# First layer: the q product from tokens without their shift, and the shift's part added as a product of its own

## The chip, the cores and the metric

The kernel runs on one core of a Trainium2 chip. The metric is the device time of one execution in microseconds (us). Engines are named as in the profile: PE (TensorE matmul), PEld (its weight loads), DVE (VectorE), ACT (ScalarE), POOL (GpSimd), SP (the queue that issues the weight DMAs).

## The reference, cut to what matters

Two token streams of 256 tokens by 1024 channels, x and ctx, pass through the first layer. The kernel goes on through expert layers and a second block; the change touches the first layer's start.

```python
sh1, sc1, g1, sh2, sc2, g2 = split(silu(c) @ ada_w[0] + ada_b[0], 6)   # 1024 -> 6 x 1024; c for x, c_ctx for ctx
h = rms_norm(x, norm_mix[0]) * (1 + sc1) + sh1                       # shift sh1, scale sc1
proj = h @ ev_w_in                                                   # q 512 | k 512 | v 512 | z 512 | gates 16 | pool 512
qkv = silu(dw_conv(proj[:, :1536], conv_w))                          # conv of width 3 over tokens
# q and z, pool only of x; k, v and the gates of both streams
```

The convolution is linear and q is linear in h, so q = (h without shift) @ w + (shift @ w), the second term being the same for every token.

## The kernel before, in words

Activations lie with channels on the partitions: `hT` is 8 tiles k of 128 channels by 512 columns, 0 to 255 for x and 256 to 511 for ctx. Weights stream in chunks of 2 MB (1024 rows by 512 columns), issued by SP in the order of the list `stream` (L443 to L453) into a ring of four slots; a chunk waits for the release of the one that held its slot four places earlier. The 24 chunks `ada_w` give the modulation vectors: `ada_mm` (L603) is a product with 32 columns (in the profile 16 matmul records at L613), ACT copies its bank to `PART` (`ada_copy`, L1707), `ada_turn` (L618) transposes it on PE in four pieces (L571), and `ada_bias` (L2230) sums and adds the bias on DVE into `MOD`. The first four chunks hold shift tiles 0 to 3, shift 4 to 7, scale 0 to 3, scale 4 to 7. SP waits for x and ctx, loaded by the ACT queue (L1628), before it issues the third (L1464 to L1466).

Order of the start: ACT squares the tokens, DVE finishes the root and scales them (L2287 to L2294), PE turns them into `hT` (L639 to L644), and PE does four ada products with their turns (L638, L645 to L650). DVE then scales and shifts the eight x tiles (L2310). The q product reads them: two quarters (m = 0, 1; a quarter is 128 output columns) as plain f32 products (L680), two as three products each of split operands (`first_product`, L669). A split operand is a high part in fp32r made by ACT and a low part, the rest, made by DVE: for weights `high` (L1610, 128x1024) and `split` (L2188, 128x1024), for the tokens L1725 and L1731 on ACT and `first_low` (L2314) on DVE. The first quarter of k, over 512 columns, needs the split of all 16 token tiles. ACT also scales and shifts the ctx tiles of `hT` (L1736), which the gates' product reads later.

Behind it, `late_vectors` (L652) turns some vectors, `ada_step` (L662) does an ada product, and k, v, z, pool follow, with an `ada_step` between each. For each output tile t ACT copies the bank to `CB` (L1759), DVE convolves it: one `tensor_scalar` (L2339) and two `scalar_tensor_tensor` (L2182), then ACT applies silu. DVE does the weights' low part and this work in one fixed order (L2329 to L2343). The mixer's order is written out in `mixer_steps` (L69); its step `ada_product` is an `ada_step`. POOL makes masks at the start and waits from L1545 for the mixer.

## Time and profile before

| | us |
|---|---|
| median of 3 runs (1290.58 to 1293.01) | 1290.7 |
| the profiled execution's own time | 1291.09 |
| its span, first to last instruction | 1289.1 |
| PE busy in the span | 1121.6 (87%) |
| DVE busy | 630.3 (49%) |
| ACT busy | 452.4 (35%) |
| POOL busy | 78.4 (6%) |

Times in rows are microseconds from the span's start. A timeline row has start, length, engine, line, operation, out<-in, shapes and the count of merged instructions; in brackets the idle time before it and what ended it. A length can overlap the next start, since an engine begins an instruction before the one in front has left it. A groups row has busy time, and the mean of one in ns. PEclk 1.00 is 2.4 GHz and 0.50 is 1.2 GHz.

### The profile page before, as it was taken

Reading aid. Unit: us, or ns where it says so; the run is one execution under the profiler, and the core shown is the slowest. Engines: PE = TensorE matmul, PEld = TensorE weight load, DVE = VectorE, ACT = ScalarE, POOL = GpSimd, SP = SyncE. Lnnn points to the kernel's source line nnn. Section 1 sums busy time; section 2 is a strip of 40 time slices with the busy share of each in tenths; the row PEclk is TensorE's granted clock in tenths of the full one; section 3 lists DMA queues with packets and bytes.
Section 4 is the critical chain, followed back from the end, with each engine's and each line's share of the span. In section 5 each row is a group of like instructions: output and inputs, shape, how many; then the busy total and the mean of one; then the engine's idle time right before and its main releaser. Section 6 shows DMA issues by size and latency. Waiting matters only on the chain.

```text
span 1289.1 us, 19518 instructions
## 1 busy us (share of the span) xinstructions
PE 1121.6 (87%) x8166; PEld 840.5 (65%) x8166; DVE 630.3 (49%) x1175; ACT 452.4 (35%) x835; POOL 78.4 (6%) x118
## 2 busy tenths in 40 slices
PE   5899999999996757589999766669999999999998
PEld 2677667896842313169995222316899879999886
DVE  4655876656530102056654010103886378656774
ACT  3535534322410000034332000002565668453553
POOL 3000124540000000000000000000100000000000
PEclk8999999999998878899999887879999999999999
DMA  9937766109989999995778999999454313453300
GB/s 325 337 131 264 276 227 217 67 15 390 420 345 421 421 421 421 420 384 178 291 289 335 421 420 421 422 421 391 137 196 143 126 60 132 146 181 131 131 18 33
DMA packets 104187, 339.17 MB, mean 263 GB/s; under 512 B 7849, under 2 KB 10774, under 8 KB 81574
## 3 DMA queue, kind: packets, MB, share of 16 engines
q1 hardware_dynamic: 97408, 334.51, 66.9%
q10 hardware_dynamic: 6694, 3.43, 1.0%
q8 instruction: 65, 1.06, 0.3%
q14 instruction: 20, 0.16, 0.0%
HBM read 336.88 MB, written 1.05 MB: 262 GB/s over the span
## 4 chain that ended last, share of the span: by engine, by line
PE 62%; DMA 15%; SPq 10%; DVE 8%; ACT 3%; issue 2%; ACTq 0%; DVEq 0%
PE bank L708 8%; PE bank L710 8%; PE bank L709 8%; SPq L1439 5%; SPq L1450 4%; PE bank L1072 4%; PE bank L613 3%; DMA arena<-in_w_gate_dram 3%; DMA arena<-in_w_up_dram 3%; DMA weight_ring<-in_w_up_dram 3%; DMA weight_ring<-in_w_gate_dram 3%; DVE arena L2179 2%; DMA weight_ring<-in_w_down_dram 2%; PE bank L690 2%; PE bank L691 2%
## 5 line engine op out<-in xcount | busy, mean ns | idle before, releaser
L2179 DVE TENSOR_TENSOR weights_low<-weight_ring,weights_high 128x1024 fp32r<-128x1024 f32 x150 | 183.4, 1224 | 121.9 <-ACT weights_high L1621 121.4
L1621 ACT ACTIVATE weights_high<-weight_ring 128x1024 fp32r<-128x1024 f32 x150 | 158.3, 1057 | 192.5 <-PE bank L710 179.2
L708 PE MATMUL bank<-input_high,weights_high 128*128 128x272 f32 (+1 forms) x672 | 195.2, 290 | 4.8 <-DVE input_low L2179 2.3
L710 PE MATMUL bank<-input_high,weights_low 128*128 128x272 f32 (+1 forms) x672 | 191.8, 285 | 0.0
L709 PE MATMUL bank<-input_low,weights_high 128*128 128x272 f32 (+1 forms) x672 | 191.3, 285 | 0.0
L708 PEld LDWEIGHTS bank<-input_high,weights_high 128*128 128x128 f32 x672 | 126.6, 188 | 9.2 <-issue 4.9
L2179 DVE TENSOR_TENSOR arena<-arena,bank 128x512 f32<-128x512 f32 (+1 forms) x38 | 24.6, 651 | 219.8 <-PE bank L1072 206.4
L710 PEld LDWEIGHTS bank<-input_high,weights_low 128*128 128x128 f32 x672 | 126.8, 189 | 0.0
L709 PEld LDWEIGHTS bank<-input_low,weights_high 128*128 128x128 f32 x672 | 126.5, 188 | 0.1
L708 PE MATMUL bank<-raw_high,weights_high 128*128 128x272 f32 (+1 forms) x320 | 93.1, 291 | 2.0 <-DVE weights_low L2179 2.0
L710 PE MATMUL bank<-raw_high,weights_low 128*128 128x272 f32 (+1 forms) x320 | 91.2, 285 | 0.0
L1072 PE MATMUL bank<-weight_ring,arena 128*32 128x512 f32 x448 | 61.6, 692 | 28.0 <-DMA weight_ring<-in_w_up_dram 18.1
L1072 PE MATMUL bank<-arena 128*32 128x512 f32 x384 | 57.5, 744 | 27.1 <-DMA arena<-in_w_up_dram 16.7
L709 PE MATMUL bank<-raw_low,weights_high 128*128 128x256 f32 (+1 forms) x256 | 72.8, 284 | 0.0
L2179 DVE TENSOR_TENSOR arena<-arena 128x272 f32<-128x272 f32 (+12 forms) x94 | 52.7, 568 | 20.8 <-ACT arena L2007 9.0
L708 PEld LDWEIGHTS bank<-raw_high,weights_high 128*128 128x128 f32 x320 | 60.1, 188 | 3.7 <-DVE weights_low L2179 3.2
L710 PEld LDWEIGHTS bank<-raw_high,weights_low 128*128 128x128 f32 x320 | 60.3, 188 | 0.0
L1072 PEld LDWEIGHTS bank<-weight_ring,arena 128*32 128x32 f32 x448 | 16.0, 125 | 67.2 <-issue 65.3
L613 PE MATMUL bank<-weight_ring,silu_c 128*32 128x512 f32 x384 | 49.2, 633 | 11.4 <-DMA weight_ring<-in_ada_w_dram 11.4
L1072 PE MATMUL bank<-expert_slots,arena 128*32 128x512 f32 x192 | 33.8, 866 | 28.3 <-DMA expert_slots<-in_w_up_dram 18.4
L2182 DVE SCALAR_TENSOR_TENSOR arena<-arena,vectors 128x272 f32<-128x272 f32 (+2 forms) x106 | 56.9, 539 | 2.9
L2182 DVE SCALAR_TENSOR_TENSOR residual<-bank,modulation,residual 128x256 f32<-128x256 f32 x80 | 36.1, 484 | 42.1 <-PE bank L998 25.7
(469 smaller groups left out, 1970.6 us busy)
## 6 DMA issues: line engine op xcount, KB each, us to landing
weight_ring<-in_ada_w_dram SPq DMA_DIRECT2D x24, 2048.0 KB, 10.2
weight_ring<-in_w_gate_dram SPq DMA_DIRECT2D x16, 2048.0 KB, 24.5
arena<-in_w_down_dram SPq DMA_DIRECT2D x16, 2048.0 KB, 32.7
arena<-in_w_gate_dram SPq DMA_DIRECT2D x12, 2048.0 KB, 21.6
arena<-in_w_up_dram SPq DMA_DIRECT2D x12, 2048.0 KB, 33.0
weight_ring<-in_w_up_dram SPq DMA_DIRECT2D x12, 2048.0 KB, 27.5
weight_ring<-in_even_w_in_dram SPq DMA_DIRECT2D x9, 2048.0 KB, 9.0
expert_slots<-in_w_up_dram SPq DMA_DIRECT2D x8, 2048.0 KB, 32.7
```

Of the source, the lines that this page charges most:

```text
L613: mm = pe.matmul(b[j:j + 32, :], CS[:, 2 * k:2 * k + 32], w[:, k, :], start=k < 4, stop=k >= 4)
L690: pe.matmul(b[:, 0:width], hi[:, k, :], XHI1[:, k, 0:width], start=k == 0, stop=False)
L691: pe.matmul(b[:, 0:width], hi[:, k, :], XLO1[:, k, 0:width], start=False, stop=False)
L708: pe.matmul(b[:, 0:width], hi[:, k, :], high[:, k, t0:t0 + width], start=k == 0, stop=False)
L709: pe.matmul(b[:, 0:width], hi[:, k, :], low[:, k, t0:t0 + width], start=False, stop=False)
L710: mm = pe.matmul(b[:, 0:width], lo[:, k, :], high[:, k, t0:t0 + width], start=False, stop=k == KD - 1)
L1072: mm = pe.matmul(b[32 * e:32 * e + 32, :], XG[:, 2 * q + k, 32 * e:32 * e + 32], w[e][:, k if by_quarter else 2 * (q % 2) + k, :], start=q ...
L1439: sp.dma_start(dst, src).then_inc(landed[slot_of(cn)], 16)
L1450: sp.dma_start(dst.rearrange("p (e n) -> p e n", e=2), src).then_inc(landed[slot_of(cn)], 16)
L1621: act.activation(WHI[:, j % 2], quarter_of(j), ACT.Copy).then_inc(weights_high, 1)
L2179: return dve.tensor_tensor(out_, a, b, op)
L2182: return dve.scalar_tensor_tensor(out_, a, s, b, op0, op1)
```

## The change

The scale chunks are loaded first, then q's weights, then ctx (by SP, in two DMAs), then the two shift chunks. Token work is done stream by stream. DVE only scales the x tiles; q's four quarters are all plain f32 products of unshifted tokens. Behind the third quarter PE turns the ctx tokens and does the two shift products; the token split with the shift folded in (ACT `Identity` with bias, DVE `scalar_tensor_tensor`) starts then, under the fourth. `shift_product` multiplies the shift with q's weights, which keeps q's slot until then; the result is copied, turned, summed and added by DVE to the four q tiles in `CB` ahead of their convolution. The shift is added to `hT` itself by POOL, in four operations of 128x1024, behind the whole split. The small DMAs (gates' weights and two vectors) move from 16 us to behind the split on ACT's queue. The ada step ahead of k goes behind k's second quarter. In the mixer, an `ada_product` does its product first and the turn of the one before it behind that; the last warm-up of PE is put ahead of the last turn.

```diff
-        stream = ada_src[0:4]
+        ada_order = [2, 3, 0, 1] + list(range(4, 24))
-        for src in ((ev, 0), (ev, 512), None, (ev, 1024), None, None, (ev, QKV), (ev, QKV + 512 + 16), None, None, None):
+        for src in (None, None, (ev, 0), None, None, (ev, 512), None, (ev, 1024), None, None, (ev, QKV), (ev, QKV + 512 + 16),
+                    None, None, None):
...
-            ada_mm()
-            for tt in range(2 * TT):
...
-            for i in range(3):
+            for tt in range(TT):
+                token_turns(tt)
+            for i in range(2):
+                warm(3)
                 ada_mm()
-                pe.wait_ge(scalar_drained, ada["copied"] - 1)
-                ada_turn()
-            pe.wait_ge(scalar_drained, ada["copied"])
-            ada_turn()
+                ada_turn_now()
...
+            def ada_step(turn_behind=False):
+                copied, turned = ada["copied"], ada["turned"] < ada["next"]
+                if turn_behind:
+                    ada_mm()
+                if turned:
+                    pe.wait_ge(scalar_drained, copied)
                     ada_turn()
+                if not turn_behind:
+                    ada_mm()
...
-                        if (i, m) in ((0, 2), (1, 0)):
-                            pe.wait_ge(first_split, KD * i + k + 1)
+                        if (i, m) == (1, 0):
+                            pe.wait_ge(first_split, 2 * k + 2)
...
+            def unshifted_product(between):
+                cn = W_EV[0]
+                arrive(cn)
+                for m in range(4):
+                    b = s_open()
+                    for k in range(KD):
+                        if m == 0:
+                            pe.wait_ge(h_scaled, k + 1)
+                        mm = pe.matmul(b[:, 0:T], chunk(cn)[:, k, m * P:m * P + P], hT[:, k, 0:T], start=k == 0, stop=k == KD - 1)
+                    s_close(mm, ("qkv", m))
+                    between(m)
+            def shift_product():
+                cn = W_EV[0]
+                pe.wait_ge(shift_ready, 2)
+                shifts = MOD[:, 0, :, :].rearrange("p c r -> p (c r)")
+                b = s_open()
+                for k in range(KD):
+                    j = 32 * (k % 4)
+                    mm = pe.matmul(b[j:j + 32, :], shifts[:, 2 * k:2 * k + 32], chunk(cn)[:, k, :], start=k < 4, stop=k >= 4)
+                released[cn] = (scalar_filled, s_close(mm, "shift_parts"))
...
+            def after_q(m):
+                if m == 2:
+                    for tt in (2, 3):
+                        token_turns(tt)
+                    ada_mm()
+                    ada_mm()
+                    pe.wait_ge(scalar_drained, ada["copied"] - 1)
+                    ada_turn()
+                if m == 3:
+                    ada_turn_now()
+            def after_k(m):
+                if m == 0:
+                    shift_turn()
+                if m == 1:
+                    ada_step()
             warm(4)
-            first_product(0, 0, T, s_open, s_close, "qkv")
+            unshifted_product(after_q)
             late_vectors()
-            ada_step()
-            first_product(1, 4, 2 * T, s_open, s_close, "qkv")
+            shift_product()
+            first_product(1, 4, 2 * T, s_open, s_close, "qkv", between=after_k)
...
-                    ada_step()
+                    ada_step(turn_behind=kind == "ada_product")
...
+            warm(3)
             pe.wait_ge(scalar_drained, ada["copied"])
             ada_turn()
...
+            pool.wait_ge(first_split, 2 * KD)
+            for r in range(2):
+                for k in (0, 4):
+                    h = hT[:, k:k + 4, r * T:r * T + T]
+                    pool.tensor_tensor(h, h, last(MOD[:, 0, k:k + 4, r], T), ALU.add).then_inc(h_shifted, 1)
...
+            act.wait_ge(shift_ready, 1)
+            act.wait_ge(context_scaled, 1)
             for k in range(KD):
+                if k == 2:
+                    high()
+                if k == 4:
+                    conv_input(3, 1)
+                    b = take()
+                    drained(act.activation(XH[:, :, 0:META], bank(b, KD, META), ACT.Copy))
+                    act.wait_ge(shift_ready, 2)
+                for r, done in enumerate((h_ready, context_high)):
+                    s = slice(r * T, r * T + T)
+                    act.activation(XHI1[:, k, s], hT[:, k, s], ACT.Identity, bias=MOD[:, 0, k, r:r + 1]).then_inc(done, 1)
+                if k == 4:
+                    b = take()
+                    drained(act.activation(QBP, b[:, :], ACT.Copy))
             high()
...
+            h = hT[:, :, T:2 * T]
+            tt(h, h, last(gain[:, :, 1], T), MUL).then_inc(context_scaled, 1)
             for k in range(KD):
+                if k % 4 == 0:
+                    ada_bias(shift_ready, k // 4 + 1)
+                if k == 2:
+                    split()
                 first_low(k, 0, h_ready)
+                first_low(k, 1, context_high)
             split()
             vec_copies((1, 2))
             tt(gain_sq, vec("norm_final", 0, 8), vec("norm_final", 0, 8), MUL)
+            b = take()
+            parts = b[:, :].rearrange("p (f q s) -> p f s q", f=4, q=4)[:, :, 0, :]
+            drained(dve.reduce_sum(QB, parts, AX.X), True)
+            dve.wait_ge(scalar_drained, mark[("qkv", 3)])
+            v = CB[:, :, 0, 1:1 + T]
+            then(tt(v, v, last(QB, T), ADD))
             for t in range(12):
-                if t >= 3:
+                if t == 2 or t > 4:
                     split()
```

## Rows read from the trace of the kernel before

**Rows 1.** The chain that ended last, 0 to 62 us: start, length, what
```profile
12.38 22.51 DMA weight_ring<-in_ada_w_dram
...
34.93 3.24 PE bank L613 x16
```
**Rows 2.** Busy by stretch: PE, PEld, DVE, ACT, POOL, PEclk, DMA share, GB/s
```profile
59.00:81.40 22.40, 22.40 (x103) 17.95 (x105) 14.79 (x22) 7.69 (x13) 0.00 (x0) 1.00 0.46 167
...
121.70:145.00 23.30, 23.30 (x175) 16.53 (x175) 15.77 (x47) 11.78 (x22) 0.00 (x0) 1.00 0.45 153
```
**Rows 3.** Timeline of PE, first 42 us
```profile
19.62 4.15 PE L571 MATMUL bank<-ident,arena 128*128 128x128 f32 x32
...
28.57 1.92 PE L613 MATMUL bank<-weight_ring,silu_c 128*32 128x512 f32 x16 [2.36 <-DMA weight_ring<-in_ada_w_dram]
...
34.93 3.24 PE L613 MATMUL bank<-weight_ring,silu_c 128*32 128x512 f32 x16 [3.85 <-DMA weight_ring<-in_ada_w_dram]
...
39.50 0.66 PE L571 MATMUL bank<-ident,ada_partials 128*128 128x128 f32 x4 [0.75 <-ACT ada_partials L1711]
39.99 2.00 PE L579 MATMUL bank<-upper_then_ones 128*128 128x272 f32 x8
41.83 7.07 PE L680 MATMUL bank<-arena,weight_ring 128*128 128x256 f32 x32
```
**Rows 4.** One stretch, PE alone: length, PE busy, PEclk, DMA share, GB/s
```profile
32.00:36.00 4.00, 1.07 (x8) 0.78 1.05 387
```
**Rows 5.** Timeline of DVE, first 60 us
```profile
10.44 1.29 DVE L2226 COPY residual<-bank 128x512 f32<-128x512 f32 x2 [0.16 <-PE bank L597]
...
14.81 2.78 DVE L2294 TENSOR_SCALAR arena<-arena 128x1024 f32<-128x1024 f32 x4
...
57.15 0.35 DVE L2339 TENSOR_SCALAR arena<-arena,vectors 128x256 f32<-128x256 f32 x1
57.53 1.01 DVE L2182 SCALAR_TENSOR_TENSOR arena<-arena,vectors 128x256 f32<-128x256 f32 x2
```
**Rows 6.** DMA issues, 15 to 25 us (q's chunk, issued 19.75): KB, us to landing
```profile
weight_ring<-in_ev_w_in_dram SPq DMA_DIRECT2D x1, 2048.0 KB, 20.6
```
**Rows 7.** Timeline of PE: k's first product, its last, v's first
```profile
58.31 0.50 PE L690 MATMUL bank<-first_input_high,weights_high 128*128 128x512 f32 x1
...
80.57 0.40 PE L692 MATMUL bank<-first_input_high,weights_low 128*128 128x512 f32 x1
...
83.19 0.50 PE L690 MATMUL bank<-first_input_high,weights_high 128*128 128x512 f32 x1
```
**Rows 8.** Groups by form: the operations of the splits and convolutions
```profile
L2179 DVE TENSOR_TENSOR weights_low<-weight_ring,weights_high 128x1024 fp32r<-128x1024 f32 x150 | 183.4, 1224 | 121.9 <-ACT weights_high L1621 121.4
L1621 ACT ACTIVATE weights_high<-weight_ring 128x1024 fp32r<-128x1024 f32 x150 | 158.3, 1057 | 192.5 <-PE bank L710 179.2
...
L1658 ACT ACTIVATE input_high<-arena,modulation 128x256 fp32r<-128x256 f32 x8 | 3.3, 495 | 1.3 <-DVE arena L2182 1.3
...
L2182 DVE SCALAR_TENSOR_TENSOR input_low<-arena,modulation,input_high 128x256 fp32r<-128x256 f32 x8 | 3.3, 481 | 0.0
...
L2182 DVE SCALAR_TENSOR_TENSOR arena<-arena,vectors 128x512 f32<-128x512 f32 x16 | 12.0, 752 | 0.6
```
**Rows 9.** POOL beside DVE in the mixer: a group, then timeline rows
```profile
L1568 POOL TENSOR_TENSOR arena<-arena,small 128x512 f32<-128x512 f32 x8 | 8.5, 1064 | 0.0
...
245.72 1.05 POOL L1568 TENSOR_TENSOR arena<-arena,small 128x512 f32<-128x512 f32 x1
245.94 1.38 DVE L2179 TENSOR_TENSOR arena<-arena,small 128x512 f32<-128x512 f32 x1
246.73 1.61 POOL L1563 TENSOR_TENSOR arena<-backward_direction,arena 128x512 f32<-128x512 f32 x1
...
253.96 0.68 DVE L2179 TENSOR_TENSOR arena<-arena,small 128x512 f32<-128x512 f32 x1
```
**Rows 10.** Timeline of PE in the mixer: a turn that waits for its copy
```profile
196.16 0.66 PE L571 MATMUL bank<-ident,ada_partials 128*128 128x128 f32 x4 [0.72 <-ACT ada_partials L1711]
```

More of the change, by code:

```diff
@@ L1463, in _ @@
                     sp.wait_ge(first_vec_in, 16 * len(first_vecs))
-                if cn == 2:
-                    sp.wait_ge(x_in, 16)
-                    sp.wait_ge(ctx_in, 16)
+                if cn == 3:
+                    for i in range(TT):
+                        sp.dma_start(XIN[TT + i], ctx[0][i * P:i * P + P, :]).then_inc(ctx_in, 16)
                 free_slot(cn)
@@ L1508, in _ @@
             then(pool.memset(GW[:, KD, :], 0.0))
+            then(pool.memset(MOD[:, 0, :, :], 0.0))
             pool.iota(SLOTN, pattern=[[1, CAP]], base=1, channel_multiplier=0,
@@ L1627, in _ @@
                 act.dma_start(VEC[r:r + k, g, :], vec_src[name]).then_inc(first_vec_in, 16)
[L1628 to L1629 removed]
+            for i in range(TT):
+                act.dma_start(XIN[i], x[0][i * P:i * P + P, :]).then_inc(x_in, 16)
             logs()
@@ L1718, in _ @@
                     drained(act.activation(hT[:, 4 * kh:4 * kh + 4, tt * P:tt * P + P], bank(b, 4, P), ACT.Copy))
-            for _ in range(3):
-                ada_copy()
-            for k in range(KD):
-                scaled_tiles[0] += 1
-                act.wait_ge(h_scaled, scaled_tiles[0])
-                act.activation(XHI1[:, k, 0:T], hT[:, k, 0:T], ACT.Copy).then_inc(h_ready, 1)
-            high()
-            high()
-            for half in range(2):
-                ks = range(4 * half, 4 * half + 4)
-                for k in ks:
-                    act.activation(XHI1[:, k, T:2 * T], hT[:, k, T:2 * T], ACT.Identity, scale=gain[:, k, 1:2],
-                                   bias=MOD[:, 0, k, 1:2]).then_inc(context_high, 1)
-                act.wait_ge(context_high, 4 * half + 4)
-                for k in ks:
-                    h = hT[:, k, T:2 * T]
-                    act.activation(h, h, ACT.Identity, scale=gain[:, k, 1:2], bias=MOD[:, 0, k, 1:2]).then_inc(context_scaled, 1)
@@ L1737, in _, with conv_input @@
-            high()
+            def conv_input(t, w):
+                b = take()
+                drained(act.activation(CB[:, t % 4, 0:w, 1:1 + T], bank(b, w, T), ACT.Copy))
+            hidden_tokens(1)
+            for _ in range(2):
+                ada_copy()
+            act.wait_ge(edges_ready, 1)
+            conv_input(0, 1)
+            act.wait_ge(ctx_in, 16 * TT)
+            token_squares_of(1, context_squares)
+            conv_input(1, 1)
+            conv_input(2, 1)
+            hidden_tokens(3)
@@ L2236, in ada_bias @@
                 drained(dve.reduce_sum(MODS, parts, AX.X), True)
-                then(tt(MOD[:, ly, c0:c0 + 4, :], MODS, last(vec("ada_b", 48 * ly + c0, 4), 2), ADD))
+                ins = tt(MOD[:, ly, c0:c0 + 4, :], MODS, last(vec("ada_b", 48 * ly + c0, 4), 2), ADD)
+                if signal is None:
+                    then(ins)
+                else:
+                    ins.then_inc(signal, 1)
+                    dve.wait_ge(signal, value)
                 ada[0] += 1
@@ L2298, in _, with first_low @@
                     drained(dve.tensor_copy(hT[:, 4 * kh:4 * kh + 4, t_ * P:t_ * P + P], bank(b, 4, P)))
-            for i in range(4):
+            def first_low(k, r, signal):
+                dve.wait_ge(signal, k + 1)
+                s = slice(r * T, r * T + T)
+                stt(XLO1[:, k, s], hT[:, k, s], MOD[:, 0, k, r:r + 1], XHI1[:, k, s].bitcast(F32), ADD, SUB).then_inc(first_split, 1)
+            token_roots(0)
+            for _ in range(2):
                 ada_bias()
```

150 lines of the change are left out of this document (71 added, 79 removed).

## The prediction

> **What bounds the kernel now.** I read the chain of waits first, since the change lies in the first 80 us. There the end is set by the load of the fourth modulation chunk, which lands at 34.9, and by its product on PE [rows 1]. Next the stretches: from 59 us to 145 us PE is busy without a gap at 2.4 GHz [rows 2], so whatever moves v's first product earlier moves everything behind it, and the one number to forecast is that start. It is at 83.19; k runs from 58.31 to 80.8 [rows 7], 5.6 us a quarter, and an ada step of turn and product (2.4 us) follows. So k starts 23 us after the chunk has landed, and the time between goes to q, to the split of 16 token tiles and to an ada step.
>
> The sum is made against the profiled execution, 1291.09 us (span 1289.1); that is 0.4 above the median, so a difference found here is put on 1290.7.
>
> **First part: until q may start.** In the new order two chunks and x stand ahead of q's weights. q's chunk lands at 19.75 + 20.6 = 40.35 [rows 6], four 2 MB chunks, x and ctx (1 MB each) having come before; a chunk takes some 5.4 us (34.9 to 40.35). Counted back from that, the second scale chunk lands near 19, q's near 25, the last shift chunk, which has the place that q had, at 40.35. PE: DVE is free at 11.73 (10.44 + 1.29), finishes the root in 0.8 and scales the first tile in 0.70; 16 turns follow from 13.3, 0.13 to 0.2 us each (4.15 for 32), to 16.5 [rows 3, 5]. A warm-up of three is 1.4 (eight records take 1.85 without the tail), an ada product 1.85, its copy and turn 1.16 (PE idles 0.72 of it [rows 10]). Twice 4.4 us gives 25.4; the warm-up of four ends at 27.25, and q starts. DVE's gain and first scaled tile are ready at 26.6.
>
> **Second part: until the split may start.** A plain quarter is 3.4 us (7.07 for two, less 0.3 of tail [rows 3]). Two quarters that were split products (24 of 0.117, 2.8 us) become plain: 0.6 more each, on PE. Three quarters end at 37.5; 16 turns of ctx (2.1) at 39.6; two products (3.7) at 43.3, past the landing at 40.35, so PE and not the DMA decides here; a turn 43.8. ACT copies the second product (0.6), DVE has the shift at 44.2, ACT starts the split at 44.5.
>
> **Third part: the split, T0.** ACT needs 0.40 for an `Identity` with bias alone (495 ns with its overlap, the row of the same form), against 0.51 for those with scale and bias, and the eight separate ones on ctx in `hT` go: 16 times 0.40 is 6.4. Between them stand a weights' high part (0.95), waits for DVE's second modulation sum behind its own part of four k (to 50.4), and the wait for `shift_product` (50.45 to 52.3) with its copy (0.6); then three k at 0.8 give 55.3. DVE follows with 0.41 an operation (481 ns [rows 8]) and ends the last low part at T0 = 55.8. PE does k's first quarter behind it as tiles come, to T0 + 0.8, where it now reached this point at 63.9. That is 7.3 us earlier, of which the ada step takes its share back, as it now comes later.
>
> **Fourth part: POOL beside DVE.** At T0 POOL starts four operations of 128x1024 that read two SBUF operands. Of 128x512, one takes 1.06, with starts 1.0 apart, so one of 128x1024 is 2.0 by the starts, 2.1 by the lengths, as an estimate from twice the elements; I take 2.0, since they follow one another. While such a one runs, DVE's operation with two SBUF inputs waits: 1.38 us instead of 0.68, and the next of POOL behind it 1.61; they alternate [rows 9]. DVE's order behind T0 is just made of these: the low part of k's second quarter (1.15 without its overlap [rows 8]), which waits for ACT until T0 + 0.5 and so finds POOL first; `gain_sq`; the addition to the four q tiles (1.15); the convolutions of two q tiles (1.3 each [rows 5]); the low part for the third quarter. So, from T0: POOL to 2.1, low part to 3.3, POOL to 5.3, `gain_sq`, POOL to 7.4, addition to 8.6, POOL to 10.6, convolutions to 12.9, low part 14.05. PE: second quarter 3.3 to 8.9, ada product to 10.8, then it waits 3.3 us for that low part. Third quarter 14.1 to 19.7; DVE does two q tiles, one k tile (two of 0.71 and one of 0.47 are 2.0) and the low part by 19.85; fourth quarter to 25.5, ada step 2.4: v starts at T0 + 27.9 = 83.7, which is 0.5 later than now. Copies from PSUM lie under POOL's operations at no cost. If that cover went, they would cost 0.3 to 0.5 each.
>
> By the Trainium skill ("SBUF — State Buffer", Who interferes with whom) a `tensor_scalar` in its two-port mode contends with GpSimd as well; no row shows one beside a reading POOL operation, and by it the first convolution's multiplication, too, waits for POOL's fourth, for another 0.35.
>
> **Clock.** After 2.4 us without work PE did an ada product in 1.92, at the full clock; after 4 us in 3.24, the granted clock having gone to 1.2 GHz (0.78 in the mean [rows 3, 4]). The wait of 3.3 us lies between: nothing, or 1.4. I take 0.7.
>
> **What moves at no cost.** The ada step behind k's second quarter is the same work in another place: its chunk is issued at 52.4, behind the release by `shift_product`, and a chunk that meets an idle DMA needs under 10, so it is there before 64; v's follows 5.4 later, needed at 75 for its high part. The small DMAs issued on ACT at T0 + 0.5 cost its queue some 1.9 us ahead of the high part that DVE wants at T0 + 12.9. POOL's `memset` of MOD lies under the wait for x. The gates' product waits for POOL's last operation at 66, and comes near 120.
>
> **Mixer.** Of the five `ada_product` steps one follows another directly; there PE's idle 0.72 [rows 10] goes: 0.7 gained. The last warm-up over the last copy: 0.2 (the token split on DVE is next, 0.2 behind). The others have their copy long done.
>
> **Sum.** v starts 0.5 later, clock 0.7, mixer -0.9: +0.3, so 1291.0. What a measurement can tell from no change is 0.2%, 2.6 us.
>
> **Rivals.** *DVE isn't held up (or POOL's operations find other gaps).* Then the low part is done at T0 + 1.65, the second quarter at 7.3, the third follows behind the ada product at 9.15, the fourth ends at 20.35 and v starts at T0 + 22.75 = 78.55: -4.6, with the mixer -5.5, 1285.2, and no clock cost. For it: no row has POOL's operations of 1024 elements or this access pattern (four tiles of 256), and the page of the profile does not name POOL in the chain at all. Against it: the rows beside POOL end with POOL, at either side. 20 in 100. *Half of it:* POOL starts behind DVE's low part or its operations are shorter (1.7), and the early part runs 1.5 us quicker as turns go at 0.13 and a warm-up hides in waiting: 1288.0. 12 in 100.
>
> *Slower: the early part at 1.2 GHz.* In the new order the first ada product comes on 16 turns and a warm-up behind a pause of 2.4 us, with the granted clock at 1.2 GHz as in the row of the product of 3.24. If it stays there until the second product is done, the turns take 1.2 more, the warm-up 1.4 and one product 1.4, and, as PE is the bound up to the split, 3 to 4 us pass on to T0: 1294.6. It decides from the point at which q starts later than 30. By the Trainium skill ("TensorE: Matmul & The Clock Gate", The HAM clock gate) the rate is the throttled one by default and activity releases it, so the warm-ups placed there should end this early; the rows agree with the two levels (0.78 in a stretch with an idle part, 1.00 behind), and none shows this order of work. 15 in 100. *Slower by ordering:* DVE falls behind on q's convolutions further than its order shows and PE waits in the fourth quarter too: 2 us, 1293. 5 in 100. *That the change doesn't do what it says* (q's start still waits for a fourth chunk): the stream's order is plain in the list, under 1 in 100.
>
> **How the numbers follow.** The sum has 48 in 100, with its own range 1288.6 to 1293.3: the clock's 0 to 1.4, POOL's 2.0 to 2.1 (four times), 1.2 us either way for the start. 8 times in 10 needs the case without hold-up and stops short of the slow start: 1284.9 to 1293.6. Faster by over 0.2% (under 1288.1): the first rival, half of the second, a tail of the sum, 0.29. Slower by over 0.2% (over 1293.3): 0.19. Within: 0.52.
>
> **What would show it.** Right: q's first plain product near 27, its third quarter's end near 37.5; ACT's first `Identity` at 44.5; the last first_input_low near 56; four POOL operations of 2 us from there, the weights_low between the first and second at 2 us or more instead of 1.22, the addition of 128x1024 as long; PE idle some 3 us ahead of k's third quarter, released by DVE; v's first product at 83 to 85. Wrong: DVE's operations at their usual lengths beside POOL's; PE with no wait in k; v's first product under 80 or over 86; the split released by a DMA.

## The result, and the profile after

The changed kernel takes 1293.16 us (median of 16 runs, 1291.66 to 1297.43), against 1290.8 for the kernel before (16 runs beside them). The ratio is 1.0022, with a 95% interval of 1.0014 to 1.0030: 1.8 to 3.9 us slower. The forecast was 1291.0, a change too small to tell from none. The measured time is inside its range of 1284.9 to 1293.6, but 2.2 us above it, and the change costs time where it was to cost nothing. One run of a later variant, h_all, took 1454.98 us at a mean granted clock of 0.738 and is in no ratio.

| profiled execution, us | before | after |
|---|---|---|
| own time | 1291.09 | 1293.07 |
| span | 1289.1 | 1291.3 |
| PE busy | 1121.6 | 1130.0 |
| DVE busy | 630.3 | 638.1 |
| POOL busy | 78.4 | 88.8 |
| q's first product | 41.83 | 29.29 |
| v's first product | 83.19 | 85.82 |

So v's first product came 2.63 us later, where the sum had put it 0.5 later. PE's timeline from 10 us to 90 us, the rows that answer to [rows 3, 7] (start, length, engine, line, operation, shapes, count; in brackets the idle time ahead and what ended it):

```profile
13.75 3.68 PE L575 MATMUL bank<-ident,arena 128*128 128x128 f32 x16 [2.36 <-DVE arena L2377]
17.22 2.57 PE L583 MATMUL bank<-upper_then_ones 128*128 128x272 f32 x6
19.72 1.92 PE L617 MATMUL bank<-weight_ring,silu_c 128*32 128x512 f32 x16
...
27.46 2.00 PE L583 MATMUL bank<-upper_then_ones 128*128 128x272 f32 x8
29.29 10.52 PE L713 MATMUL bank<-arena,weight_ring 128*128 128x256 f32 x48
...
41.49 3.64 PE L617 MATMUL bank<-weight_ring,silu_c 128*32 128x512 f32 x32
...
52.15 1.92 PE L725 MATMUL bank<-weight_ring,modulation 128*32 128x512 f32 x16 [1.59 <-DVE modulation L2254]
...
60.77 0.50 PE L695 MATMUL bank<-first_input_high,weights_high 128*128 128x512 f32 x1 [0.51 <-DVE weights_low L2254]
...
66.51 1.93 PE L617 MATMUL bank<-weight_ring,silu_c 128*32 128x512 f32 x16
70.85 0.80 PE L695 MATMUL bank<-first_input_high,weights_high 128*128 128x512 f32 x1 [2.42 <-DVE weights_low L2254]
71.44 0.63 PE L696 MATMUL bank<-first_input_low,weights_high 128*128 128x512 f32 x1
...
85.82 0.50 PE L695 MATMUL bank<-first_input_high,weights_high 128*128 128x512 f32 x1
```

The reader is to see three things. The 16 turns take 3.68 and the warm-up of three (six records) 2.57, where the same warm-up takes 1.54 at the full clock: PE worked at 1.2 GHz up to the first ada product, which at 1.92 is back at 2.4 GHz. Later PE idles 1.59 us ahead of the shift product, 0.51 ahead of k's second quarter and 2.42 ahead of its third. And the products that follow the last wait are longer, 0.63 where the stretch around them has 0.39.

The windows of the stretch of [rows 2], of the wait and of what follows it (columns as in [rows 2]):

```profile
59.00:81.40 22.40, 19.48 (x88) 14.21 (x87) 20.41 (x28) 7.73 (x12) 8.16 (x4) 0.92 0.83 286
...
68.00:71.00 3.00, 0.58 (x6) 0.15 (x1) 2.93 (x6) 2.58 (x5) 0.00 (x0) 0.92 1.05 394
71.00:74.00 3.00, 3.00 (x8) 2.36 (x9) 2.82 (x8) 2.24 (x5) 0.00 (x0) 0.52 0.92 337
...
121.70:145.00 23.30, 23.30 (x176) 14.96 (x175) 15.33 (x44) 13.18 (x25) 0.00 (x0) 1.00 0.46 155
```

Where PE was busy for all of 22.4 us at PEclk 1.00 before, it is busy for 19.48 at 0.92. From 68 to 71 it works 0.58 us, and from 71 to 74 it works all the time at 0.52, the level of 1.2 GHz. The stretch from 121.7 on is as before.

POOL and DVE behind T0, which is 57.65 here (55.17 and 2.48, the end of the last low part of the tokens), each in its own timeline:

```profile
57.74 1.90 POOL L1605 TENSOR_TENSOR arena<-arena,modulation 128x1024 f32<-128x1024 f32 x1 [41.67 <-DVE first_input_low L2257]
59.59 2.88 POOL L1605 TENSOR_TENSOR arena<-arena,modulation 128x1024 f32<-128x1024 f32 x1
62.43 1.89 POOL L1605 TENSOR_TENSOR arena<-arena,modulation 128x1024 f32<-128x1024 f32 x1
64.29 2.87 POOL L1605 TENSOR_TENSOR arena<-arena,modulation 128x1024 f32<-128x1024 f32 x1
```

```profile
58.11 2.60 DVE L2254 TENSOR_TENSOR weights_low<-weight_ring,weights_high 128x1024 fp32r<-128x1024 f32 x1 [0.46 <-ACT weights_high L1683]
...
61.12 1.37 DVE L2254 TENSOR_TENSOR small<-vectors 128x8 f32<-128x8 f32 x1
...
62.61 2.80 DVE L2254 TENSOR_TENSOR arena<-arena,small 128x1024 f32<-128x1024 f32 x1
65.44 1.87 DVE L2435 TENSOR_SCALAR arena<-arena,vectors 128x256 f32<-128x256 f32 x1
...
68.27 0.35 DVE L2435 TENSOR_SCALAR arena<-arena,vectors 128x256 f32<-128x256 f32 x1
...
69.58 1.22 DVE L2254 TENSOR_TENSOR weights_low<-weight_ring,weights_high 128x1024 fp32r<-128x1024 f32 x1
```

The low part that stands among POOL's four operations takes 2.60, the one behind them 1.22; the sum of eight columns takes 1.37; the addition of 128x1024 takes 2.80. The first `tensor_scalar` of the convolutions takes 1.87, the second, behind POOL's end at 67.16, takes 0.35. POOL is held in turn: its first and third operation take 1.90 and 1.89, its second and fourth, which meet DVE's low part and DVE's addition, 2.88 and 2.87. The chain that ended last goes through just these (start, length, what):

```profile
57.13 0.96 ACT weights_high L1683
58.11 2.60 DVE weights_low L2254
...
62.61 2.81 DVE arena L2254
65.44 1.88 DVE arena L2435
...
69.66 1.15 DVE weights_low L2254
70.85 0.80 PE bank L695
```

POOL isn't named in the chain: its hold on DVE shows as long DVE operations alone.

### The profile page after: what moved, and what is told of

Its sections match the earlier page's. It is cut to its first block, busy times and chain, and to the rows that moved or that the text cites. A ratio compares the mean times of both kernels' runs of the same rounds, so it can differ in the third digit from the quotient of the medians.

```text
span 1291.3 us, 19554 instructions
## 1 busy us (share of the span) xinstructions
PE 1130.0 (88%) x8182; PEld 846.8 (66%) x8182; DVE 638.1 (49%) x1180; ACT 447.3 (35%) x828; POOL 88.8 (7%) x123
## 3 DMA queue, kind: packets, MB, share of 16 engines
q10 hardware_dynamic: 6438, 2.38, 0.8%
## 4 chain that ended last, share of the span: by engine, by line
PE 63%; DMA 13%; SPq 10%; DVE 9%; ACT 3%; issue 2%; ACTq 0%; DVEq 0%
PE bank L743 8%; PE bank L745 8%; PE bank L744 8%; SPq L1494 5%; SPq L1505 4%; PE bank L1127 4%; PE bank L617 3%; DVE arena L2254 3%; DMA weight_ring<-in_w_up_dram 3%; DMA weight_ring<-in_w_gate_dram 3%; DMA arena<-in_w_up_dram 2%; DMA arena<-in_w_gate_dram 2%; DMA weight_ring<-in_w_down_dram 2%; PE bank L575 2%; PE bank L916 2%
## 5 line engine op out<-in xcount | busy, mean ns | idle before, releaser
L2254 DVE TENSOR_TENSOR arena<-arena 128x272 f32<-128x272 f32 (+12 forms) x96 | 55.7, 587 | 21.3 <-ACT arena L2082 9.0
L1127 PEld LDWEIGHTS bank<-arena 128*32 128x32 f32 x384 | 14.3, 132 | 63.6 <-issue 61.0
```

What stands on the lines that cost most here:

```text
L1127: mm = pe.matmul(b[32 * e:32 * e + 32, :], XG[:, 2 * q + k, 32 * e:32 * e + 32], w[e][:, k if by_quarter else 2 * (q % 2) + k, :], start=q ...
L2254: return dve.tensor_tensor(out_, a, b, op)
```

## The experiments

The times of q, T0 and v are from one profiled execution of each kernel: q the start of its first product, T0 the end of the last low part of the tokens, v the start of its first product. Medians and ratios to the kernel before are from 5 to 16 runs, and the kernel before had 1290.65 to 1290.91 beside them. The ratio is not that of the medians: where a kernel's runs fall into groups (a_pool_late has five from 1284.9 to 1286.5 and six from 1288.9 to 1289.7), a median can move by more than 1 us while the ratio stays. "Fall at 50" and "at 70" say whether the granted clock went to 1.2 GHz around the shift product and around k's third quarter.

| kernel | q | T0 - q | v - T0 | v | fall at 50 | at 70 | median | ratio, 95% interval |
|---|---|---|---|---|---|---|---|---|
| changed | 29.29 | 28.36 | 28.17 | 85.82 | no | yes | 1293.16 | 1.0014 to 1.0030 |
| a_pool_late | 27.74 | 29.97 | 23.52 | 81.23 | yes | no | 1288.91 | 0.9962 to 0.9984 |
| b_no_pool_add | 28.00 | 29.99 | 23.53 | 81.52 | yes | no | 1287.39 | 0.9968 to 0.9989 |
| c_warm_first | 26.71 | 30.07 | 28.35 | 85.13 | yes | yes | 1294.22 | 1.0018 to 1.0042 |
| e_both | 26.04 | 29.27 | 24.51 | 79.82 | yes | no | 1285.45 | 0.9950 to 0.9975 |
| f_no_turn_behind | 30.08 | 28.36 | 28.25 | 86.69 | no | yes | 1293.81 | 1.0007 to 1.0025 |
| d_no_first_warm | 26.65 | 30.09 | 28.35 | 85.09 | yes | yes | 1291.85 | 0.9999 to 1.0019 |
| j_late_warm | 27.62 | 28.36 | 23.53 | 79.51 | no | no | 1287.57 | 0.9968 to 0.9992 |
| h_all | 26.69 | 28.46 | 23.57 | 78.72 | no | no | 1285.41 | 0.9950 to 0.9973 |
| k_fill_stall | 29.10 | 28.35 | 26.96 | 84.41 | no | no | 1292.42 | 1.0001 to 1.0019 |
| g_warm_shift | 27.64 | 28.36 | 26.96 | 82.96 | no | no | 1292.26 | 1.0003 to 1.0026 |
| l_first_shift | 26.76 | 28.46 | 28.36 | 83.58 | no | yes | 1290.66 | 0.9989 to 1.0007 |
| m_order | 25.99 | 26.77 | 23.49 | 76.25 | no | no | 1284.72 | 0.9940 to 0.9964 |

The two middle columns take few values, and each value goes with a cause. T0 - q is 28.35 to 28.46 without a fall at 50 and 29.97 to 30.09 with a full one. v - T0 is 23.5 without POOL beside DVE, 26.96 with it, and 28.2 to 28.4 when the clock falls as well. (e_both, where the fall came late, and m_order, with another order on DVE, have values of their own.) The span less v's start is 1203.5 to 1210.0 in these executions, so one execution's own time can't tell the small effects apart; the starts can, and the medians say whether they arrive at the end.

Much of that spread comes from stretches at 1.2 GHz behind v. From v's start to the first product behind the mixer's last ada step (325.05 in the changed kernel) it is 237.6 to 237.7 us in the three executions of the new mixer order without such a stretch (a_pool_late, b_no_pool_add, e_both), 238.6 to 238.7 with one at 167 to 176 us, 239.2 to 239.3 with one at 311 to 313, and 240.2 to 240.4 with both. It is 240.8 in h_all, where one of 6.8 us began at 305.6, and 241.8 in j_late_warm, with one at 171 and one of 6.8 us at 307.2.

**POOL's additions, moved and left out.** In a_pool_late each of the four waits for a later low part of the weights:

```diff
-            for r in range(2):
-                for k in (0, 4):
-                    h = hT[:, k:k + 4, r * T:r * T + T]
+            for i in range(4):
+                r, k = i // 2, 4 * (i % 2)
+                pool.wait_ge(weights_split, 5 + i)
+                h = hT[:, k:k + 4, r * T:r * T + T]
```

> The changed kernel, but each of POOL's four additions waits for one more weights' low part of v's product (the 5th to the 8th), so none runs beside DVE's work behind the token split. Theory (POOL's operations hold up DVE's): the low part for k's second quarter takes 1.2 us again and not 2.6, the addition to the q tiles 1.2 and not 2.8, PE no longer idles ahead of k's third quarter (2.4 us now), and v's first product comes at 80.5 to 81.5 in place of 85.8; some 4.8 us under the changed kernel, 1288.3, ratio to before 0.998. Rival (DVE's own order behind the split is too long whatever POOL does): v's first product stays within 1 us of 85.8 and the time at 1293.

DVE in this run, the rows that answer to those at 58.11, 62.61 and 65.44 above, and POOL:

```profile
58.17 1.23 DVE L2255 TENSOR_TENSOR weights_low<-weight_ring,weights_high 128x1024 fp32r<-128x1024 f32 x1 [0.46 <-ACT weights_high L1684]
...
60.57 1.23 DVE L2255 TENSOR_TENSOR arena<-arena,small 128x1024 f32<-128x1024 f32 x1
61.84 0.35 DVE L2436 TENSOR_SCALAR arena<-arena,vectors 128x256 f32<-128x256 f32 x1
...
64.45 1.22 DVE L2255 TENSOR_TENSOR weights_low<-weight_ring,weights_high 128x1024 fp32r<-128x1024 f32 x1
```

```profile
76.87 2.87 POOL L1606 TENSOR_TENSOR arena<-arena,modulation 128x1024 f32<-128x1024 f32 x1 [60.61 <-DVE weights_low L2255]
82.71 2.07 POOL L1606 TENSOR_TENSOR arena<-arena,modulation 128x1024 f32<-128x1024 f32 x1 [2.97 <-DVE weights_low L2255]
```

The same operations take 1.23, 1.23 and 0.35 instead of 2.60, 2.80 and 1.87, and PE has no wait in k's second and third quarter. With T0 at nearly the same place (57.71 and 57.65) v starts 4.59 us earlier, the median is 4.25 lower, and the two intervals are clear of each other. POOL's operation takes 2.07 where DVE does not hold it.

b_no_pool_add leaves the additions out, so that the gates' product reads tokens without their shift:

```diff
-            pool.wait_ge(first_split, 2 * KD)
-            for r in range(2):
-                for k in (0, 4):
-                    h = hT[:, k:k + 4, r * T:r * T + T]
-                    pool.tensor_tensor(h, h, last(MOD[:, 0, k:k + 4, r], T), ALU.add).then_inc(h_shifted, 1)
-            pe.wait_ge(h_shifted, 4)
```

> The changed kernel without POOL's four additions and without the wait for them: the gates' product then reads tokens without their shift (this part of the computation is left out). Theory (POOL holds up DVE): as the kernel with the additions moved behind, v's first product at 80.5 to 81.5, the time 1288.3 (0.998 of before); if it is faster than that one by over 1 us, the moved additions still cost something. Rival (DVE's own order): 1293, v's first product at 85.8.

v - T0 is 23.53, the same as with the additions late. The median is 1.5 lower than a_pool_late's, more than the 1 us that was to mean a cost, but the ratio points the other way (0.9978 against 0.9973) and the two intervals overlap for the most part. So late additions have no cost that shows, and nearly all that made them dear was their place.

**The start of PE.** c_warm_first puts a warm-up of four ahead of the turns of x, in the wait for DVE, in place of the three behind them; d_no_first_warm only leaves the three out:

```diff
+            warm(4)
             for tt in range(TT):
                 token_turns(tt)
             for i in range(2):
-                warm(3)
+                if i:
+                    warm(3)
                 ada_mm()
```

> The changed kernel, with PE's first warm-up (now three products between the turns of x and the first modulation product) put ahead of these turns, where PE is idle for 2.4 us, and four products long. Theory (the start is late by 2 us against my sum as turns and warm-up run at 1.2 GHz): the 16 turns take 2.1 us in place of 3.7 and the warm-up's 2.5 us lies in the idle time, q's first product comes near 25.5 in place of 29.3, and v's first product, as PE is the bound up to the split, 2 to 3.8 earlier (but not under 41.5 us for the last shift product, which the DMA sets at 40.4): 1290.5, ratio 0.9998. Rival (the clock falls whatever stands there, by a pause that is already over): the turns still take 3.7, the gain is only the 1.5 to 2.5 us of the warm-up moved. Second rival (the DMA of the last shift chunk is what ends last): q starts earlier and the shift product waits for its chunk: nothing gained behind 44.

> The changed kernel without the warm-up of three ahead of the first ada product. Theory: at 1.2 GHz the warm-up costs 2.57 us and buys nothing if the product would wait for no one else, so q starts up to 2.6 earlier; if the clock is still at 1.2 GHz then, the product takes 3.2 to 3.6 instead of 1.92 and the next turns are slow, so q starts 0.5 to 1.3 earlier, near 28.4, and POOL's hold-up on DVE remains (v's first product 84.6 to 85.8; 1292 to 1293). Rival: the second product waits for its DMA (lands near 22) and q's start is unmoved: 1293.2.

PE's timeline of c_warm_first:

```profile
11.20 2.38 PE L583 MATMUL bank<-upper_then_ones 128*128 128x272 f32 x8
13.79 1.97 PE L575 MATMUL bank<-ident,arena 128*128 128x128 f32 x16 [0.21 <-DVE arena L2379]
15.69 1.93 PE L617 MATMUL bank<-weight_ring,silu_c 128*32 128x512 f32 x16
...
21.29 1.92 PE L617 MATMUL bank<-weight_ring,silu_c 128*32 128x512 f32 x16 [0.93 <-DMA weight_ring<-in_ada_w_dram]
...
26.71 10.63 PE L715 MATMUL bank<-arena,weight_ring 128*128 128x256 f32 x48 [0.29 <-DMA weight_ring<-in_ev_w_in_dram]
...
69.97 0.79 PE L697 MATMUL bank<-first_input_high,weights_high 128*128 128x512 f32 x1 [2.40 <-DVE weights_low L2256]
```

The turns take 1.97 instead of 3.68, and q starts 2.6 earlier; waits for the second chunk (0.93) and for q's (0.29) keep it from being more. Only 0.7 of that arrives at v, and nothing at the end (1290.5 was expected, 1294.22 measured): the clock now falls in the 1.6 us wait ahead of the shift product, which takes 3.5 instead of 1.92, and again in the wait for DVE. d_no_first_warm came to the same start: the clock's records of this execution show 2.4 GHz from 12.0, so its turns took 1.97 with no warm-up ahead, and q started at 26.65. Its median is 1.3 under the changed kernel's and c_warm_first's is 1.1 over it, at one and the same v, and the two intervals meet only at their ends, so what lies between 85 us and the end hides this size of effect. That d_no_first_warm's turns were quick was chance: up to their end its code is that of the changed kernel. Over all kernels, the turns took 1.91 to 1.97 in the five executions with the warm-up ahead of them, and without it 2.91 to 3.68 in seven of eight.

e_both has both edits, late additions and the warm-up ahead:

> Both edits together: POOL's additions moved behind and the first warm-up ahead of the turns. Theory: the two gains lie one behind the other on the same chain and add up: v's first product near 78, 1285.5, ratio 0.996. Rival (they overlap, as DVE or the DMA takes over as bound): no faster than the better of the two alone, 1288.

It is at 1285.45, as expected, though v came at 79.82 and not near 78. It is 8.8 under c_warm_first, more than the 5.3 by which v starts earlier. The clock fell here too, but later (50.4, inside the shift product, 2.55), and the slow products reached into k's first quarter: so 29.27 and 24.51 in the table, in place of 30.0 and 23.5, and the same sum.

**The clock in PE's waits.** Three kernels fill a wait without taking it away. k_fill_stall puts a warm-up of four behind the ada product in k:

```diff
                 if m == 1:
                     ada_step()
+                    warm(4)
```

> The changed kernel with a warm-up of four (2.0 us) behind the ada product in k, in the 2.4 us that PE waits there for DVE's low part. The wait itself stays. Theory: the granted clock fell at 70.5 because of that wait, and the fall cost 1.7 beside the wait; with work in it the third quarter runs at 2.4 GHz, v's first product is at 84.1 instead of 85.8, and the time is 1291.5 to 1291.9 against 1293.2. Rival: the fall has another cause (the stretch comes anyway), the third quarter still shows products of 0.43 instead of 0.23, v starts at 85.8 and the time is 1293.2.

```profile
66.32 1.92 PE L617 MATMUL bank<-weight_ring,silu_c 128*32 128x512 f32 x16
68.18 2.10 PE L583 MATMUL bank<-upper_then_ones 128*128 128x272 f32 x8
70.64 0.50 PE L695 MATMUL bank<-first_input_high,weights_high 128*128 128x512 f32 x1 [0.37 <-DVE weights_low L2255]
```

PE still gets the low part 2.5 us late, but the third quarter's product takes 0.50 and not 0.80, and v - T0 is 26.96 instead of 28.17: the fall had cost 1.2. v starts 1.41 earlier (1.7 was expected); the median is 0.74 lower, and the intervals overlap.

g_warm_shift and j_late_warm have a warm-up of three in the wait ahead of the shift product, the first in the changed kernel, the second on top of a_pool_late:

```diff
             late_vectors()
+            warm(3)
             shift_product()
```

> The changed kernel with a warm-up of three ahead of the shift product alone; POOL's additions where the change put them. Theory: in the changed kernel the clock did not fall at this place, so there is nothing to win: v's first product at 85.8, the wait of 2.4 for DVE and the fall at 70.5 as before, 1293.2. Rival: the idle 1.6 counts together with the later wait, and without it the fall at 70.5 does not come: v at 84.1, 1291.5.

> POOL's additions late, as in the run that spread them over v's quarters, and a warm-up of three in the 1.6 us that PE idles ahead of the shift product. Theory: that idle time is what let the granted clock fall at 50.5 (shift product 3.53 instead of 1.92); with work in it the product takes 1.92 and k and v start 1.6 earlier: v's first product near 79.6, 1287.3 against 1288.9 for the same kernel without this warm-up. Rival: the clock falls there anyway or falls at the next short idle time, and the 1.6 is paid somewhere else before 90 us: 1288.9, v's first product at 81.

j_late_warm, then g_warm_shift:

```profile
48.73 1.54 PE L583 MATMUL bank<-upper_then_ones 128*128 128x272 f32 x6
50.48 1.92 PE L725 MATMUL bank<-weight_ring,modulation 128*32 128x512 f32 x16 [0.21 <-DVE modulation L2256]
```

```profile
69.20 0.50 PE L695 MATMUL bank<-first_input_high,weights_high 128*128 128x512 f32 x1 [2.38 <-DVE weights_low L2255]
```

In j_late_warm the shift product takes 1.92, and T0 - q is 28.36 instead of 29.97; v is 1.7 earlier, as its theory had it. The end does not show it: the median is 1.3 lower, but the ratio is higher (0.9980 against 0.9973), and this execution had two stretches at 1.2 GHz between v and 320 us where a_pool_late's had none. g_warm_shift waited 2.38 us for DVE with nothing in it, and its clock didn't fall. So a wait of this length can lower the clock, and mostly did: it fell in five of the six executions that had it empty (not in this one), and in five of the eight with an empty 1.6 to 1.8 us ahead of the shift product. Where the wait was filled it never fell: once for the wait for DVE, four times for the one ahead of the shift product. The rival in g_warm_shift's expectation, that the two waits count together, fits its profile but not l_first_shift's, where the first is filled and the clock falls at the second all the same. Its own theory, that nothing was to be won, missed for v (82.96 against 85.8); the median is 0.9 under the changed kernel's, with intervals that overlap.

l_first_shift (c_warm_first and the warm-up ahead of the shift product) and h_all (that with late additions) complete the set:

> The changed kernel with the warm-up of PE ahead of the turns of x (q starts 2.6 earlier) and a warm-up of three ahead of the shift product; POOL's additions where the change put them. Theory: the earlier q start gave only 0.7 at v's first product because the clock fell at 49.5 and cost 1.6; with that idle time filled T0 comes 0.6 to 1.6 earlier and so does all behind it: v at 83.5 to 84.5, 1291.0 to 1292.5; the wait of 2.4 for DVE stays, and the fall at 70 with it. Rival: DVE and ACT set T0 whatever PE's clock is: v at 85.1, as without it, 1293 to 1294.

> POOL's additions late, the warm-up of PE ahead of the turns of x instead of behind them, and a warm-up of three ahead of the shift product. Theory: without the fall of the clock at 50.4 the shift product takes 1.92 instead of 2.55, and the first four products of k 0.23 instead of 0.43 each, 1.6 in all: v's first product at 78.2 instead of 79.8, 1283.8 against 1285.4. Rival: that time is hidden by the token split, which DVE ends at 55.3, and only 0.6 or nothing comes through: 1284.8 to 1285.4.

In l_first_shift v starts at 83.58, 1.55 before c_warm_first, and the intervals are clear of each other; it is no longer slower than the kernel before. The theory held, and the rival, that ACT and DVE set T0 whatever the clock is, fell. In h_all v starts 1.1 before e_both's, yet both medians are 1285.4 (1283.8 was expected): in the profiled execution of h_all the clock fell for 6.8 us at 305.6, where e_both has no fall, and by 320 us h_all is 2.0 behind. That execution took 1289.77, well over its median, so why the medians are equal stays open.

**The mixer's order.** f_no_turn_behind:

```diff
-                    ada_step(turn_behind=kind == "ada_product")
+                    ada_step()
```

> The changed kernel with the mixer's order of an ada step as it was before (turn first, product behind it). Theory: the mixer's part of the change gave back 0.7 us at the one place where one product follows another directly, so this kernel is 0.7 us slower than the changed one, 1293.9, with v's first product unmoved at 85.8 and an idle of 0.7 ahead of a turn near 198. Rival: the offset of the two kernels moves between 147 us and 204 us by the granted clock's stretches and not by this order; then the idle is there again and the time is 1293.2, and the offset at 203 us is as in the changed kernel (0.5 to 1).

The turn that answers to [rows 10], in the changed kernel and in this one:

```profile
196.28 0.66 PE L575 MATMUL bank<-ident,ada_partials 128*128 128x128 f32 x4
```

```profile
198.68 0.65 PE L575 MATMUL bank<-ident,ada_partials 128*128 128x128 f32 x4 [0.72 <-ACT ada_partials L1772]
```

The idle 0.72 is back and the median is 0.65 higher. v started 0.87 later in this execution through a later start (x landed 0.8 later), which is another reason to look at the idle time and not at the ends. The ratio points the other way (1.0016 against 1.0022) and the intervals overlap, so the ends show nothing. The starts do: with no stretch at 1.2 GHz between, it is 238.7 us here from v to the first product behind the mixer, and 237.6 to 237.7 in the kernels with the new order.

**DVE's order in the split.** In m_order, on e_both, DVE makes the second sum of the shift ahead of the weights' low part:

```diff
-                if k % 4 == 0:
-                    ada_bias(shift_ready, k // 4 + 1)
+                if k in (0, 2):
+                    ada_bias(shift_ready, k // 2 + 1)
                 if k == 2:
                     split()
```

> POOL's additions late, the warm-up ahead of the turns of x, and DVE's second sum of the shift ahead of the low part of the weights instead of behind four k of the token split. The sum is ready at 46.9 instead of 49.2. Theory: the shift product starts when the vectors are turned, at 47.6 to 48.1 instead of 49.2, PE has 0.5 or less of idle ahead of it, the clock does not fall, and k's first product starts at 50.0 instead of 51.7; the split on ACT and DVE then sets the end of k's first quarter, about 1 earlier than 58.3: v's first product at 78.5, 1284.0 to 1284.5 against 1285.4. Rival: ACT's chain (second input of the split loop, the copies) sets it and nothing is won: v at 79.8, 1285.4.

```profile
47.19 1.92 PE L727 MATMUL bank<-weight_ring,modulation 128*32 128x512 f32 x16
```

```profile
46.58 0.17 DVE L2257 TENSOR_TENSOR modulation<-small,vectors 128x8 f32<-128x8 f32 x1
46.78 1.23 DVE L2257 TENSOR_TENSOR weights_low<-weight_ring,weights_high 128x1024 fp32r<-128x1024 f32 x1
```

The sum stands ahead of the low part, the shift product follows the vectors' turns with no wait, and T0 - q falls to 26.77. v starts at 76.25 (78.5 was expected), 3.6 before e_both and 9.6 before the changed kernel. The median is 1284.72, and the ratio to the kernel before 0.9952 (0.9940 to 0.9964): 5.9 us faster than 1290.65. Of the 3.6 us against e_both only 0.7 are in the median, and its interval overlaps e_both's. In the profiled execution a stretch at 1.2 GHz at 167 us, which e_both's lacks, takes back 0.9 of them by 315 us; where the rest went is open.

## Why the prediction was right or wrong

**Until q may start: this step failed.** I had q at 27.25; it started at 29.29, and in this execution all of the miss up to T0 is here. In its steps: the turns began at 13.75 (I had 13.3), took 3.47 from start to start (3.2), the warm-up 2.50 (1.4), so of the 2.04 some 1.4 is work at 1.2 GHz that the sum had quicker. I had used 0.13 to 0.2 us a turn and the full clock for the warm-up, and had put 1.2 GHz into a rival. At 1.2 GHz a turn is 0.22, and at the full clock 0.12 (1.97 for 16 in c_warm_first). The slower rival was half right: turns and warm-up were slow, by 2.6 together (at the full clock they take 1.90 and 1.47 from start to start), but the clock was back for the first product, which that rival had slow as well. Its point, q later than 30, was set too far out, since a later q passed on in full. By the Trainium skill ("TensorE: Matmul & The Clock Gate", The HAM clock gate) the point of release varies between executions of one kernel: the seven executions with the changed kernel's early code agree, with q from 27.62 to 30.08 (some of it x landing 0.8 later).

**From q to T0: right.** 28.55 by my steps, 28.36 measured. The products ended at 45.06 (I had 43.3, 1.8 late as q was), ACT's first `Identity` came at 46.31 (44.5), and PE and not the DMA decided. What I left out was the clock at the 1.6 us ahead of the shift product, a term put at nothing without a reason: the fall cost 1.6 to 1.7 in four executions and 0.9 in a fifth, and those were ones in which q had started at 28.0 or before. So T0 was at 57.45 to 58.44 in all five executions with this early code and the wait empty, whichever of the two had happened. So the early part met 1.2 GHz in either case, and the sum had it in neither (T0 at 55.8). In l_first_shift, where both places are filled, T0 is at 55.22, v at 83.58 and the median at 1290.66, close to the forecast of 1291.0. That the median of the changed kernel is slower by this, and not just one profile, is what these five executions and l_first_shift suggest.

**POOL beside DVE: right in mechanism, 0.9 too dear.** Low part, `gain_sq`, addition and convolutions were held, in that order, as forecast. From T0, I had the low part to 3.3 (3.06), the addition to 8.6 (7.76), POOL to 10.6 (9.5), the low part for the third quarter at 14.05 (13.15). Two full DVE operations did stand between POOL's four, as I had them, but all were shorter: POOL's took 1.85 from start to start where nothing held them (I had 2.0), and DVE's two held it for 1.0 each (1.2), 9.4 us in all. PE idled 0.51 and 2.42, not 3.3. Without a fall v follows at T0 + 26.96, where I had 27.9. The hold-up is 3.45 by itself (26.96 less 23.5). The rival without hold-up had T0 + 22.75 and would have been 0.75 too cheap; it is what late additions give.

The Trainium skill's rule ("SBUF — State Buffer", Who interferes with whom) that a `tensor_scalar` contends with GpSimd too was set aside, since no row showed it. It holds here: 1.87 instead of 0.35, ending 0.15 behind POOL's fourth operation. I had put 0.35 on it; it cost about 1.5, though in the sum it lies where I had only let POOL's time pass.

**Clock: the term existed, and 0.7 was too low.** I took the mean of nothing and 1.4; the fall came and cost 1.2 (28.17 less 26.96), in five of six executions.

**Mixer: 0.7 right, 0.2 wrong.** The idle 0.72 went. At the last warm-up the change gained nothing. PE in the kernel before, then in the changed one:

```profile
322.52 0.39 PE L708 MATMUL bank<-input_high,weights_high 128*128 128x256 f32 x1
```

```profile
322.56 1.54 PE L583 MATMUL bank<-upper_then_ones 128*128 128x272 f32 x6
323.94 0.60 PE L575 MATMUL bank<-ident,ada_partials 128*128 128x128 f32 x4
325.05 0.35 PE L743 MATMUL bank<-input_high,weights_high 128*128 128x256 f32 x1 [0.51 <-DVE input_low L2254]
```

The warm-up lies over the copy now, but the first product of the next part then waits 0.51 for DVE's `input_low`. From the start of the last ada step (its turn at 317.59 before, its product at 320.22 after) to this first product it was 4.93 and is 4.83, and in f_no_turn_behind, with the moved warm-up and the old order, it is 4.93 (320.46 to 325.39). In both kernels the product starts 0.57 behind DVE's first `input_low` (321.95 before, 324.48 after), so DVE set this place already, and I had put its slack at 0.2. For the mixer as a whole the 0.7 stands: from v to this product it was 239.3 before, with one stretch at 1.2 GHz at 174 us, and 238.6 to 238.7 in the new order with one such stretch near there.

**The sum.** q 2.04 late, T0 - q 0.19 less, POOL 0.94 less, clock 0.5 more: v at 85.82, where the forecast with its clock term had 84.4. That is 1.4, and the last warm-up's 0.2 makes 1.6, against 2.2 between the medians and the forecast; 0.6 stays open. So the term of the sum that was mis-sized is the first part, the start of q, and the clock in it, with the fall ahead of the shift product as its other face. The two other errors nearly cancelled (POOL 0.9 too dear, the clock in k and the mixer 0.7 too cheap), and that is luck. That the rest is no larger is luck in part too, since the executions differ by up to 6.5 us in what lies behind v.

## What to carry to other kernels

Put POOL's operations with two SBUF inputs where DVE has slack, not at the moment that releases them: the same four operations cost 3.45 us at T0 and nothing that shows 20 us later. A wait of PE of 1.6 to 2.4 us cost its length and, in 10 of 14 cases, a stretch at 1.2 GHz behind it (0.9 to 1.7 us). So try a warm-up of the wait's length in each such wait that can't be taken away, and ahead of the first real work, not behind it; at the end of the kernel only l_first_shift, against c_warm_first, showed the gain beyond doubt. When a late engine is fed by several steps, split its start into differences (q, T0 - q, v - T0) over a few variants; for one cause each took the same value within 0.2 us, while medians of equal v differed by 2. For what lies behind, compare executions with the same stretches at 1.2 GHz.

## What the runs showed of the hardware

- DVE's `tensor_scalar` of 128x256 f32, from SBUF to SBUF, took 1.87 us beside POOL's two-input addition, against 0.35 alone, and a `tensor_tensor` with eight columns took 1.37 against 0.17.
- POOL's `tensor_tensor` of 128x1024 f32 with a broadcast operand took 1.89 to 2.08 where DVE did not hold it and 2.88 and 2.87 where it met DVE's low part and addition. The one at 76.87 in a_pool_late took 2.87 as well: it began while DVE's `memset` of 128x1280 ran (76.58 to 77.70) and ended 2.04 behind it, and so in all five kernels with late additions (2.87 to 2.89). That the `memset` held it is the likely reading and wasn't shown by an experiment, since this operation is also the first of the four each time. In turn DVE's two `scalar_tensor_tensor` of 128x512 took 3.05 beside each of the late operations, against 1.54.
- After 2.4 us without PE work the clock fell in five of six executions and after 1.6 to 1.8 us in five of eight; before the change the wait of 2.36 [rows 3] was followed by a product at full clock and the one of 3.85 by a slow one. The length alone doesn't decide.
- The clock's records of an execution begin somewhere, at 19.3 us in the changed kernel. Ahead of that the windows view gives full clock, while the turns' 3.68 us show 1.2 GHz, so lengths are the safer witness there. The window of the turns in the changed kernel:

```profile
13.70:17.20 3.50, 3.45 (x16) 3.46 (x17) 2.07 (x3) 0.59 (x1) 2.09 (x8) 1.00 1.06 379
```
